# Down projection grouped with its single pair first, operands of the last projection made earlier, one operand sum on GpSimd

## What is computed

```python
x += concat(mLSTM heads, conv channels) @ w_out       # "out": 1024 x 1024
f = rmsnorm(x, g_ffn)
x += (silu(f @ w_gate) * (f @ w_up)) @ w_down         # 1024 -> 2816 -> 1024
e = rmsnorm(pe @ w_ple, g_ple)
x += sigmoid(x @ w_pg) * e                            # "pg": 1024 x 1024
```

## Time and profile before

| | |
|---|---|
| median of 3 runs | 2758.01 us (2756.53 to 2766.91) |
| the profiled execution's own time | 2760.44 us |
| its span in the profile | 2758.7 us |
| mean granted TensorE clock | 0.962 of full |

### The profile page before, as it was taken

The page is one execution under the profiler, slowest core; times in us unless marked ns, Lnnn a source line. Parts: engine busy times, 40 slices in busy tenths (PEclk is TensorE's granted clock), DMA queues, the critical chain, the costliest instruction groups (busy, mean ns, idle before and its releaser), DMA issues.

```text
span 2758.7 us, 41116 instructions
## 1 busy us (share of the span) xinstructions
PE 2534.1 (92%) x15882; PEld 2467.8 (89%) x15882; DVE 1456.9 (53%) x2252; ACT 956.5 (35%) x1760; POOL 1138.5 (41%) x939
## 2 busy tenths in 40 slices
PE   4999789999999879989899999988998999999998
PEld 4889778999998778989899999987898989999997
DVE  4656987554665564465642333466446564333355
ACT  4344444333333533333422222253233342222233
POOL 3566646555664534223333332333322433333233
PEclk6999899999999889999999999998999999999998
DMA  5435534444553645464544555375545555555634
GB/s 167 156 144 197 179 135 176 157 157 168 187 196 111 214 144 184 150 197 150 179 135 150 174 180 166 116 230 159 178 146 187 168 172 142 162 173 173 205 100 154
DMA packets 306309, 456.46 MB, mean 165 GB/s; under 512 B 21683, under 2 KB 218596, under 8 KB 305606
## 3 DMA queue, kind: packets, MB, share of 16 engines
q1 hardware_dynamic: 239014, 269.13, 29.4%
q10 hardware_dynamic: 67104, 184.70, 21.0%
HBM read 347.44 MB, written 106.35 MB: 164 GB/s over the span
## 4 chain that ended last, share of the span: by engine, by line
PE 50%; issue 3%; DVE 3%; POOL 1%; ACT 1%; DMA 0%; DVEq 0%; POOLq 0%; ACTq 0%
PE bank L460 16%; PE bank L462 16%; PE bank L461 16%; PE bank L542 0%; POOL wring L2179 0%; DVE qlo L1442 0%; PE bank L605 0%; PE bank L553 0%; PE bank L608 0%; DVE sg L2045 0%; DVE R L1541 0%; PE bank L611 0%; PE bank L579 0%; PE bank L561 0%; PE bank L532 0%
## 5 line engine op out<-in xcount | busy, mean ns | idle before, releaser
L2179 POOL TENSOR_TENSOR wring<-wraw,wring 128x512 fp32r<-128x512 f32 x612 | 874.9, 1434 | 1330.8 <-ACT wring L1053 1318.4
L460 PE MATMUL bank<-qhi,wring 128*128 128x352 f32 (+1 forms) x3588 | 1188.8, 331 | 148.9 <-issue 71.3
L462 PE MATMUL bank<-qhi,wring 128*128 128x352 f32 (+1 forms) x3588 | 1170.4, 326 | 0.0
L461 PE MATMUL bank<-qlo,wring 128*128 128x352 f32 (+1 forms) x3588 | 1169.8, 326 | 0.0
L460 PEld LDWEIGHTS bank<-qhi,wring 128*128 128x128 f32 x3588 | 696.1, 194 | 176.2 <-issue 172.2
L461 PEld LDWEIGHTS bank<-qlo,wring 128*128 128x128 f32 x3588 | 695.9, 194 | 0.0
L462 PEld LDWEIGHTS bank<-qhi,wring 128*128 128x128 f32 x3588 | 693.7, 193 | 0.0
L1053 ACT ACTIVATE wring<-wraw 128x512 fp32r<-128x512 f32 x612 | 383.0, 629 | 874.2 <-PE bank L462 770.4
L460 PE MATMUL bank<-hid,wring 128*128 128x352 f32 (+1 forms) x960 | 307.6, 320 | 5.2 <-DVEq L1963 5.2
L462 PE MATMUL bank<-hid,wring 128*128 128x352 f32 (+1 forms) x960 | 307.1, 320 | 0.0
L461 PE MATMUL bank<-hid,wring 128*128 128x352 f32 (+1 forms) x960 | 306.1, 319 | 0.0
(11 more groups left out here) (291 smaller groups left out, 2610.9 us busy)
## 6 DMA issues: line engine op xcount, KB each, us to landing
wring<-weight_parts ACTq DMA_DIRECT2D x336, 512.0 KB, 4.1
weight_parts<-wring SPq DMA_DIRECT2D x168, 512.0 KB, 3.1
wraw<-w_down SPq DMA_DIRECT2D x33, 1024.0 KB, 5.9
wraw<-w_in SPq DMA_DIRECT2D x27, 512.0 KB, 4.5
wraw<-w_in SPq DMA_DIRECT2D x12, 1024.0 KB, 6.7
wraw<-w_gate SPq DMA_DIRECT2D x11, 1024.0 KB, 5.8
wraw<-w_up SPq DMA_DIRECT2D x11, 1024.0 KB, 5.9
wraw<-w_gate SPq DMA_DIRECT2D x22, 512.0 KB, 4.3
```

The lines of the kernel that those rows point to most:

```text
L460: nc.tensor.matmul(o, hi, mh, start=begins, stop=False, skip_group_check=True)
L461: nc.tensor.matmul(o, hi, ml, start=False, stop=False, skip_group_check=True)
L462: return nc.tensor.matmul(o, lo, mh, start=False, stop=ends, skip_group_check=True)
L2179: nc.gpsimd.tensor_tensor(wlo[e % RING][:, :].rearrange(v, k=k), w.src, whi[e % RING][:, :].rearrange(v, k=k), ALU.subtract).then_inc(lo_d ...
```

## The change

1. `down` is grouped as pair 0 alone (group 0, between gate 1 and up 1), pairs 1+2, 3+4, 5+6, 7+8 (groups 1 to 4, between gate and up of pairs 3, 5, 7, 9), and pairs 9+10 (group 5, after up 10). `down_last` and its two buffers are gone.
2. Group 5 takes both halves of the tokens in turn for each block of channels. PE's first piece waits for all of pair 10's second hidden block and half of its first.
3. Between the adds of group 5 VectorE makes T1 (now in `diff`, at k = 7), low 0 (k = 9) and low 4 (k = 12). After it come T2, low 1, operand 6, and low 5, 6, 3 as before. ScalarE's order of high parts follows.
4. In super tiles 1 and 2, operand 3 of `out`, `ffn` and `pg` is subtracted by GpSimd (`fourth_sum`) instead of VectorE: six instructions.

```diff
-    return p // 2 - 1 if p % 2 == 0 and 2 <= p < FFP - 1 else None
+    return p // 2 if p % 2 and p < FFP - 1 else None
+
+def on_pool(q, st, i):
+    return q > 0 and st != "in" and i == 3
...
+    diff = at("diff", [P, 4, NW_], F32, mix0 + 8192)
...
+                        need = (q.n, FFP - 1, 0, 1) if k % 2 else (q.n, FFP - 1, 1, None)
...
+                    if k < 2:
+                        pe.wait_ge(h_hi, HIDDEN[need])
+                        pe.wait_ge(h_lo, HIDDEN[need])
...
-                down(q, 4)
-                down_last(q)
+                down(q, 5)
...
                     if k == 7:
+                        nc.vector.tensor_tensor(diff[:, :, 0:q.N], q.X[:, 0:4, c[1]], q.X[:, 0:4, c[0]], sub).then_inc(src_ready, 1)
+                    if k == 9:
                         low_of(q, "pg", 0)
-                    if k == 11:
-                        nc.vector.tensor_tensor(R67[:, :, 0:q.N], q.X[:, 0:4, c[1]], q.X[:, 0:4, c[0]], sub).then_inc(src_ready, 1)
-                    if k == 13:
-                        low_of(q, "pg", 1)
+                    if k == 12:
+                        low_of(q, "pg", 4)
...
-                down(q, 4, range(0, 1))
-                hidden_low(q, FFP - 1, 0)
-                down(q, 4, range(1, 16))
-                down_last(q)
+                hidden_low(q, FFP - 1, 0, 1)
+                down(q, 5)
                 t_sums(q, "pg", 5)
-                low_of(q, "pg", 4)
+                low_of(q, "pg", 1)
                 t_sums(q, "pg", 6)
...
+            def fourth_sum(q, st):
+                c, N = q.blocks, q.N
+                b21, t2 = {"out": (q.U[:, 4:8, c[0]], Rz), "ffn": (mixr[:, :, 0:N], R67), "pg": (q.X[:, 4:8, c[0]], R23)}[st]
+                if freed(q.n, st, 3):
+                    pool.wait_ge(prod, freed(q.n, st, 3))
+                pool.wait_ge(src_ready, SOURCE[(q.n, st, 5)])
+                nc.gpsimd.tensor_tensor(qraw[:, 3, :, 0:N], b21, t2[:, :, 0:N], ALU.subtract).then_inc(fourth, 1)
...
+                    if j == 1 and on_pool(q.n, st, 3):
+                        fourth_sum(q, st)
```

More of the change, by code:

```diff
@@ L330, in build, with add_down @@
     ALL4, ALL2 = slice(0, 4), slice(0, 2)
+    def add_down(g):
+        if g == 0:
+            add_plain(w_down_v[:, 0:2, :], 2, D, [(ALL2, slice(256 * n, 256 * n + 256)) for n in range(4)])
+            return
+        for a in range(2):
+            add_plain(w_down_v[:, 4 * g - 2:4 * g + 2, 512 * a:512 * a + 512], 4, 512,
+                      [(ALL4, slice(P * n, P * n + P)) for n in range(4)])
     for q in supers:
@@ L356, in build @@
     operand_end = {}
-    SOURCE = counted((q, st, i) for q in range(3) for st in STAGES for i in SOURCES[st])
+    SOURCE = counted((q, st, i) for q in range(3) for st in STAGES for i in SOURCES[st] if not on_pool(q, st, i))
     HIGH = counted((q, st, i) for q in range(3) for st in STAGES for i in HIGHS[st])
     LOW = counted((q, st, i) for q in range(3) for st in STAGES for i in HIGHS[st] if i != 2)
+    FOURTH = counted((q, st) for q in (1, 2) for st in ("out", "ffn", "pg"))
     LOW2 = counted((q, st) for q in range(3) for st in STAGES)
@@ L791, in down @@
             def down(q, g):
-                e = n_entry[0]
-                pe.wait_ge(h_hi, 2 * FFP * q.n + 4 * g + 4)
-                pe.wait_ge(h_lo, 2 * FFP * q.n + 4 * g + 4)
+                e, ks = n_entry[0], 4 if g else 2
+                xs_ = range(4) if g else (2, 3)
                 for k in range(16):
                     b = q.blocks[k % 2]
[L798 to L810, removed]
+                    if g == 5:
+                        need = (q.n, FFP - 1, 0, 1) if k % 2 else (q.n, FFP - 1, 1, None)
+                    else:
+                        need = (q.n, 2 * g, 0, None)
+                    if k < 2:
+                        pe.wait_ge(h_hi, HIDDEN[need])
+                        pe.wait_ge(h_lo, HIDDEN[need])
+                    plain((q.n, "down", g, k), e + (k // 2 if g else k // 4), ks, 0 if g else k // 2 % 2, 6 + k % 2,
+                          [hid[:, 0, c, b] for c in xs_], [hid[:, 1, c, b] for c in xs_])
+                n_entry[0] += 8 if g else 4
             def pg_after(q):
@@ L1590, in t_sums @@
                     nc.vector.tensor_tensor(qraw[:, 6, :, 0:q.N], t2_, b11, sub).then_inc(src_ready, 1)
-                if which == 3:
+                if which == 3 and not on_pool(q.n, st, 3):
                     free_operand(q, st, 3)
@@ L2006, in up_corner, with down @@
                 return corner
[L2008 to L2018, removed]
+            def down(q, g):
                 c = q.blocks
                 for k in range(16):
-                    if k in (0, 2, 4, 6):
+                    if k % (2 if g else 4) == 0:
                         ahead()
-                    o, blk, bk = k % 8, c[k // 8], 6 + k % 2
-                    dve.wait_ge(*written[(q.n, "down", 5, k)])
+                    o, blk, bk = k // 2, c[k % 2], 6 + k % 2
+                    dve.wait_ge(*written[(q.n, "down", g, k)])
                     x = q.X[:, o, blk]
-                    nc.vector.tensor_tensor(x, x, bank[bk][:, 0:q.N], add).then_inc(x3, 1)
+                    last = nc.vector.tensor_tensor(x, x, bank[bk][:, 0:q.N], add)
+                    if g < 5:
+                        last.then_inc(free[bk], 1)
+                        continue
+                    last.then_inc(x3, 1)
                     dve.wait_ge(x3, 16 * q.n + k + 1)
@@ L2344, in _ @@
                     if down_before(p) is not None:
-                        for k in range(8):
+                        for k in range(8 if down_before(p) else 4):
                             ahead()
@@ L2354, in _ @@
                         pair(nothing, 0)
-                for k in range(12):
+                for k in range(8):
                     ahead()
```

79 lines of the change are left out of this document (41 added, 38 removed).

## The result

| | before | changed |
|---|---|---|
| median | 2758.44 us (4 runs, 2756.53 to 2766.91) | 2774.09 us (4 runs, 2772.64 to 2776.87) |
| ratio | | 1.0056, 95% interval 1.0042 to 1.0071 |
| profiled execution: span, clock | 2758.7 us, 0.962 | 2770.9 us, 0.964 |

A forecast was written before the change was run, and what follows sets the result against it. PE, busy 92% of the span, bounds the kernel; VectorE and GpSimd, holding each other off, set `pg`'s P3. Terms -5.2 - 5.9 + 5.8 + 2.5 + 1.1 + 6.5 = +4.8 us gave 2762.8, stated as 2762.5 us; range 2747 to 2773.

The forecast's parts named there:

- 1, bank 6: Group 0 of `down`, now after gate 1: three waits for bank 6 go, -5.2 us (bounds -5.2 to -3.5).
- 2, `down_last`: Last group of `down`: six waits behind VectorE's release go, -5.9 us (bounds -5.9 to -4).
- 3 and 4, entry of group 5 and clock: Start of group 5: wait for pair 10, 1.9 us three times, +5.8; clock loss, half of 1.7 each, +2.5 us.
- 5 and 6, the sum on GpSimd: `pg`, `out`, `ffn`, tiles 1 and 2: 3.2 us on GpSimd replace 1.54 on VectorE; +1.6 each in `pg`, +6.5 elsewhere.
- 5, the rest of `pg`: Start of `pg`: low 1 no longer delays the last adds, so T2 starts sooner, -0.7 us a tile.
- they fit: Group 0 of `down`: its short pieces (0.98 us of PE, an add of 0.52 on VectorE) would not be late.
- Rival A: `out`, `ffn`, `pg`: GpSimd's sum is free, six stages gain 1.0 to 1.6 us; total -12, 2746 us; chance 0.13.
- term 5: Start of `pg`: -0.7 us for the first tile, +0.9 for each other, +1.1 in all (bounds -6 and +5).
- Rival C: `pg`: P3 would start 12.7 us after `down` instead of 18; some 20 us less, 2742 us; chance 0.05.
- Rival B: Six stages and group 5's entry: longer PE stops lower the clock each time; 2775 us, 0.6% slower; chance 0.13.

The follow-up runs named there:

- e3: The changed kernel with the last square of the embedding's mean and its two sums made two and three steps earlier in gate 1: 2765.63 us, ratio 1.0032.
- e1: The changed kernel with the fourth operand sum back on VectorE in all stages: 2763.13 us, ratio 1.0018.
- e2: The kernel before with only the fourth operand sum of `out`, `ffn` and `pg` on GpSimd in tiles 1 and 2: 2768.85 us, ratio 1.0040.
- e8: The changed kernel with squares early and group 5's first two pieces in halves, pair 9 first; sum still on GpSimd: 2758.76 us, ratio 0.9992.
- e5: The changed kernel with the sum on VectorE, squares early and group 5's first two pieces in halves, pair 9 first: 2746.38 us, ratio 0.9945.
- e7: The changed kernel with GpSimd's sum one step later in its queue, an edit that moved nothing: 2776.77 us, ratio 1.0054.
- e9: e5 with one half piece of pair 9, in place of two, ahead of the wait for pair 10: 2747.91 us, ratio 0.9951.

## Why the prediction was wrong

It had the direction of its sum and the price of its largest part right, and missed 10.8 us in two places: 6.6 at group 0 and 4.2 at the entry of group 5.

| step of the prediction | forecast | shown |
|---|---|---|
| 1, bank 6 | -5.2 | -5.2; but group 0 does not fit: +6.6 (e3) |
| 2, `down_last` | -5.9 | -5.9, and one wait of 0.8 in its place |
| 3 and 4, entry of group 5 and clock | +5.8 and +2.5 | 7.8 of stop and some 4.7 of clock: about +12.5 |
| 5 and 6, the sum on GpSimd | 3.2 in `pg` + 6.5 | +10.5, +11, +13 (e1, e2, e8) |
| 5, the rest of `pg` | -2.1 | -2.6 to P3 (e5's trace against before) |

The clock's 4.7 is 1.4, 1.6 and 1.7 for the three tiles; the first comes from the changed kernel's stretches above, 1.8 us at 0.50 and 2 at 0.73, the others from the same stretches behind their stops. -5.2 + 6.6 - 5.9 + 0.8 + 12.5 + 10.5 - 2.6 gives +16.7, within the measured 11.6 to 19.6. The 6.6 and the 10.5 are each good to 5 us only, so that the sum comes out so near is in part luck.

**The step that failed is "they fit".** The prediction asked whether an add of 0.52 us is shorter than a piece of 0.98, and it is. It did not read what stands ahead of the first add in VectorE's queue at the new place. PE has two banks, so two pieces (1.95 us) are all the slack there is, while the queue held 1.8 us of squares' sums, stretched to 3.9, and in the first tile 2.4 of weight sums. The rule it had set up itself, that the two engines hold each other off, applies to these sums too. The bounds of term 1 (-5.2 to -3.5) were too narrow for that reason, and this alone takes the sum from 4.8 to 11.4 us.

**The loss of clock after the entry was no even chance.** The stop was taken as 1.9 us, between 1.75 with no fall and 2.02 with one, and half the loss was booked. It was 2.6, as the low part ahead of the last corner waited for a GpSimd entry. The prediction looked for such an entry only ahead of the second low part, and took 0.88 there, which held; 3.0 a tile was its upper bound. At 2.6 the loss came each time and not in half of the cases. The two stops that it chose as bounds were also too few: the same trace of before has one of 1.79 us with a fall (at 1248.05) and one of 3.12 without (at 1322.62).

**The sum's price held**, and so did its reason: mutual exclusion of whole instructions, seen in the earlier trace rows and in the 4.61 us of a VectorE sum beside GpSimd's. In tiles 1 and 2 the stages lose 1.4 to 2.3 us each in the traces (e1), where the forecast had 1.6. Its rule from the Trainium skill ("SBUF — State Buffer", section "Who interferes with whom") agrees with these rows: the instruction that came later waited for the other's end, in both directions. Rival A is out.

**`pg`** went as said in order of events: P5 follows P1 without the old 2.69 us, and P3 starts at 1822.13, 18.6 us after the last piece of `down` (forecast 18 to 19.5; the third tile has 17.9):

```profile
1822.13 0.40 PE L473 MATMUL bank<-qhi,wring 128*128 128x352 f32 x1 [0.98 <-issue]
```

From the start of the last matmul of `down` to P3 the three tiles took 22.5, 18.4 and 17.8 us before, 21.9, 18.9 and 18.2 in the changed kernel and 21.9, 17.4 and 16.8 in e5. So term 5, forecast +1.1, came as +0.4, and without its sum, forecast -2.1, as -2.6. Rival C is out.

**Rival B**, slower by the clock, gave the right size, 2775, from the wrong places. It had the entry's three full clock losses, 2.6 us over the forecast, and these came. Its 1.7 us in each of six stages did not come as such: the sum's 10.5 to 13 stands against 9.7.

What stays open: e5 gains 15 us against before. The traces explain 12 of them: -5.2, -5.9 and -2.6, with 0.8 and three entry stops of 0.77 on the other side, and 1.5 more in the third tile, where before the change P3's stop of 2.04 us took the clock down and e5's of 1.72 did not. The other 3 us are less than the interval of e5's ratio (4 to either side), and no run here separates them.

## What to carry to other kernels

When work moves to another place in an in-order program, ask of each engine that serves it what stands ahead in its queue at the new place, not only whether its own operations are shorter than their period; the slack is the number of banks times a piece. A part of a change that gives work to an idle engine has to be priced by what the two engines share, and it can be tested alone: here the idle engine cost 11 us and the rest of the change, once its two new stops were mended, gained 15. Such a test counts only if the trace shows that its edit moved what it was to move, as e7's did not. Where PE must wait for a fresh operand at the start of an accumulation, do first the part of the sum that needs only old ones, for as many banks as are free.

## What the runs showed of the hardware

- How long PE had stood mattered more than that it stood. At the entry of group 5, with the same work around it, 0.73 to 0.81 us (e5) and 1.72 or 1.73 (e9) left the clock at 1.00; 2.57 to 2.63 took it to its lower level each time (12 of 12 in the traces of the changed kernel, e1, e3 and e7), from the next matmul on or up to 1.5 us later. About 2.0 went either way: in e5 the stop of 2.01 us at 896.89 left it at 1.00 and the one of 2.01 at 1796.05 did not. Elsewhere the length alone does not tell: in the first pair of `out` it fell after 1.79 (before, at 1248.05) and stayed after 1.75 (e1, at 1250.86), and in gate 0 a stop of 3.12 us left it at 1.00 up to PE's next stop, 2.2 us on (before, at 1322.62), while one of the same length at the same place took it down at once (changed kernel, at 1328.04).
- A VectorE operation of 1.62 us took 4.61 beside one GpSimd instruction of the same shape, and GpSimd's own took 4.44 for about 3.1 of work: both had stood behind the other for a whole instruction.
- One wait more or less moves what follows by fractions of a us, and whether the clock falls in the next stage changes with it: the first stage of the second tile differs by up to 2.7 us between kernels that are alike there. A difference of that size, read from two traces in one stage, is no measurement; the first reading of the sum's price (5 to 7 us) failed on that.
